# Stick-breaking attention in a two-block network: absolute values shared between two engines, query products over steps 2 to 18, one weight chunk rounded at the stage's end

## What is computed

```
q = split_heads(u @ attn_w_q[i])
z = jnp.einsum('bhqd,bhkd->bhqk', qb, kb) * scale
causal = s_pos < t_pos
log_beta = jax.nn.log_sigmoid(z)
log_one_minus = jnp.where(causal, jax.nn.log_sigmoid(-z), 0.0)
log_remain = lax.cumsum(log_one_minus, axis=3, reverse=True) - log_one_minus
weights = jnp.where(causal, jnp.exp(log_beta + log_remain), 0.0)
o = einsum('bhqk,bhkd->bhqd', weights, vb)
h = h + o @ attn_w_o[i]
```

## Time and profile before

| | us |
|---|---|
| median of 3 runs | 2513.57 (2511.74 to 2515.11) |
| the profiled execution, its own time | 2511.76 |
| its span | 2510.0 |
| PE busy | 2483.5 (99%) |
| DVE busy | 1027.2 (41%) |
| ACT busy | 735.6 (29%) |
| POOL busy | 974.5 (39%) |

### The profile page before, as it was taken

One profiled execution on the slowest core, in us unless ns is written; L12 is line 12 of the kernel. 1 busy time (PEld: TensorE's weight loads), 2 busy tenths in 40 slices (PEclk: granted clock), 3 DMA queues, 4 the chain that ended last, 5 costly groups with the idle time before them and its releaser, 6 DMA issues.

```text
span 2510.0 us, 30052 instructions
## 1 busy us (share of the span) xinstructions
PE 2483.5 (99%) x11638; PEld 1981.9 (79%) x11638; DVE 1027.2 (41%) x1489; ACT 735.6 (29%) x963; POOL 974.5 (39%) x305
## 2 busy tenths in 40 slices
PE   9999999999999999999999999999999999999998
PEld 7777887777888888568888888888888767888887
DVE  6363615458222317974223110422321686522301
ACT  3454225523222222242222222222122453222221
POOL 3322243204444442124444444444444663444442
PEclk9999999999999999999999999999999999999999
DMA  4222132212222233512222233322223211222232
GB/s 161 100 84 84 67 118 76 93 51 84 100 100 90 85 110 103 154 36 99 100 100 80 92 113 121 131 100 100 85 92 126 83 35 51 101 100 86 84 103 79
DMA packets 42752, 235.81 MB, mean 94 GB/s; under 512 B 5552, under 2 KB 5552, under 8 KB 22448
## 3 DMA queue, kind: packets, MB, share of 16 engines
q1 hardware_dynamic: 41808, 231.55, 26.9%
q10 hardware_dynamic: 864, 3.15, 0.3%
HBM read 222.86 MB, written 6.29 MB: 91 GB/s over the span
## 4 chain that ended last, share of the span: by engine, by line
PE 70%; DVE 3%; issue 3%; POOL 1%; ACT 1%; SPq 0%; DMA 0%; DVEq 0%; ACTq 0%; POOLq 0%
PE ps L1679 22%; PE ps L1680 22%; PE ps L1681 22%; PE ps L2069 1%; PE ps L2180 1%; PE ps L2160 1%; PE ps L2197 1%; PE ps L2186 1%; POOL w_lo L579 1%; DVE w_lo L1142 0%; DVE conv_out L1508 0%; SPq L543 0%; DVE tmp L1508 0%; PE ps L2170 0%; DVE tmp L1613 0%
## 5 line engine op out<-in xcount | busy, mean ns | idle before, releaser
L579 POOL TENSOR_TENSOR w_lo<-raw,w_hi 128x2048 fp32r<-128x2048 f32 (+1 forms) x204 | 863.7, 4234 | 1365.1 <-ACT w_hi L709 1342.7
L1679 PE MATMUL ps<-x_hi,w_hi 128*128 128x512 f32 x2047 | 809.3, 395 | 2.0 <-POOL w_lo L579 1.4
L1681 PE MATMUL ps<-x_hi,w_lo 128*128 128x512 f32 x2047 | 797.8, 390 | 0.0
L1680 PE MATMUL ps<-x_lo,w_hi 128*128 128x512 f32 x2047 | 797.5, 390 | 0.0
L1679 PEld LDWEIGHTS ps<-x_hi,w_hi 128*128 128x128 f32 x2047 | 384.6, 188 | 101.4 <-issue 20.8
L709 ACT ACTIVATE w_hi<-raw 128x2048 fp32r<-128x2048 f32 (+1 forms) x215 | 375.7, 1748 | 286.3 <-PE ps L1681 281.5
L1681 PEld LDWEIGHTS ps<-x_hi,w_lo 128*128 128x128 f32 x2047 | 384.5, 188 | 81.0
L1680 PEld LDWEIGHTS ps<-x_lo,w_hi 128*128 128x128 f32 x2047 | 384.9, 188 | 77.2 <-issue 0.7
L1189 DVE TENSOR_TENSOR tmp<-ps,rms_b 128x512 f32<-128x512 f32 x88 | 60.9, 691 | 585.4 <-PE ps L1681 582.4
L1681 PE MATMUL ps<-hid_hi,w_lo 128*128 128x512 f32 x704 | 273.9, 389 | 0.0
L1679 PE MATMUL ps<-hid_hi,w_hi 128*128 128x512 f32 x704 | 273.9, 389 | 0.0
(11 more groups left out here) (255 smaller groups left out, 2436.4 us busy)
## 6 DMA issues: line engine op xcount, KB each, us to landing
raw<-in_w_up SPq DMA_DIRECT2D x88, 1024.0 KB, 4.8
raw<-in_w_down SPq DMA_DIRECT2D x64, 704.0 KB, 4.0
raw<-in_w_feat SPq DMA_DIRECT2D x22, 1024.0 KB, 4.8
raw<-in_w_pw SPq DMA_DIRECT2D x12, 1024.0 KB, 5.1
raw<-in_w_tok SPq DMA_DIRECT2D x8, 1024.0 KB, 4.9
raw<-in_w_out SPq DMA_DIRECT2D x8, 1024.0 KB, 4.8
shifted<-conv_in SPq DMA_DIRECT2D x80, 67.5 KB, 2.0
bias<-in_bias_t SPq DMA_DIRECT2D x8, 512.0 KB, 5.9
```

The lines of the kernel that those rows point to most:

```text
L579: nc.gpsimd.tensor_tensor(w_lo[:, s, 0:w], raw[:, s, 0:w], w_hi[:, s, 0:w].bitcast(f32), ALU.subtract).then_inc(lo_ready, 1)
L1679: nc.tensor.matmul(out, hi, src_hi, start=start, stop=False, skip_group_check=True)
L1680: nc.tensor.matmul(out, hi, src_lo, start=False, stop=False, skip_group_check=True)
L1681: return nc.tensor.matmul(out, lo, src_hi, start=False, stop=stop, skip_group_check=True)
```

## The change

Four edits, all in the stick-breaking stage and its end:

1. ScalarE takes the absolute value of the second head of each step (`sb_second_absolute`, function Abs, out of PSUM), ahead of the two exponentials of that step and behind the weights where those come first. DVE keeps the first head's.
2. DVE rounds the softplus with a two-input instruction (t times 1, max t, both inputs the same tile) instead of a copy.
3. The 40 query products are dealt over steps 2 to 18, and the evictions in `Q_MOVED` move with them (query tiles 6 and 7 from steps 14 and 17 to 15 and 18).
4. The second chunk of w_o is no longer rounded in quarters during steps 18 to 23 (four of `sb_high`, four of `sb_low`). ACT and POOL do it whole after the stage, as elsewhere.

```diff
--- before.py
+++ after.py
@@ -149,11 +149,11 @@
 
 
 Q_STEPS = {}
-for _t in range(5):
-    Q_STEPS[3 * _t + 3], Q_STEPS[3 * _t + 4], Q_STEPS[3 * _t + 5] = 2, 3, 3
-Q_MOVED = {3 * _t + 5: _t + 3 for _t in range(5)}
+for _first, _products in ((2, (2, 2, 2, 2)), (6, (2, 3, 3)), (9, (2, 3, 3)), (12, (2, 2, 2, 2)), (16, (3, 3, 2))):
+    Q_STEPS.update((_first + _n, _count) for _n, _count in enumerate(_products))
+Q_MOVED = {5: 3, 8: 4, 11: 5, 15: 6, 18: 7}
 PIECES = 4
-SB_HIGHS = {6: 0, 8: 1, 9: 2, 10: 3, 12: 4, 13: 5, 15: 6, 16: 7, 18: 8, 19: 9, 21: 10, 22: 11}
+SB_HIGHS = {6: 0, 8: 1, 9: 2, 10: 3, 12: 4, 13: 5, 15: 6, 16: 7}
 SB_LOWS = {i + 1: n for i, n in SB_HIGHS.items()}
 
 
@@ -442,7 +442,7 @@
 
     def sb_piece(n):
 
-        name, c = (("q", 3), ("o", 0), ("o", 1))[n // PIECES]
+        name, c = (("q", 3), ("o", 0))[n // PIECES]
         at = CHUNK // PIECES * (n % PIECES)
         return first[name] + c, c % 2, slice(at, at + CHUNK // PIECES), n % PIECES == PIECES - 1
 
@@ -689,7 +689,8 @@
             if r == 2 and pair + 2 < SB_PAIRS:
                 stage_sb(pair + 2, 2)
                 stage_sb(pair + 2, 3)
-        pool.wait_ge(lo_ready, first["o"] + 2)
+        pool.wait_ge(lo_ready, first["o"] + 1)
+        low_part("o", 0, 1)
         low_parts("o", 1)
         low_parts("up3")
         low_parts("down3")
@@ -1005,16 +1006,24 @@
                 ins = nc.scalar.activation(stick[:, u % 4, 0:n], bank[:, 0:n], ACT.Exp)
             ins.then_inc(sb_exp, 1)
 
+        def sb_second_absolute(i):
+            u, n = 2 * i + 1, sb_width(i)
+            act.wait_ge(sb_z, u + 1)
+            if u >= 6:
+                act.wait_ge(sb_soft, u - 5)
+            nc.scalar.activation(tmp[:, u % 6, 0:n], ps[:, Z_BANK[u % 6], 0:n], ACT.Abs).then_inc(act_link, 1)
+
         def sb_decay(i, e):
-            u = 2 * i + e
-            t = tmp[:, u % 6, 0:sb_width(i)]
-            act.wait_ge(sb_abs, u + 1)
+            t = tmp[:, (2 * i + e) % 6, 0:sb_width(i)]
+            if e:
+                act.wait_ge(act_link, 3 * i + 1)
+            else:
+                act.wait_ge(sb_abs, i + 1)
             nc.scalar.activation(t, t, ACT.Exp, scale=-1.0).then_inc(act_link, 1)
 
         def sb_logs(i, e):
-            u = 2 * i + e
-            t = tmp[:, u % 6, 0:sb_width(i)]
-            act.wait_ge(act_link, u + 1)
+            t = tmp[:, (2 * i + e) % 6, 0:sb_width(i)]
+            act.wait_ge(act_link, 3 * i + e + 2)
             nc.scalar.activation(t, t, ACT.Ln, bias=1.0).then_inc(sb_log, 1)
 
         def sb_high(n):
@@ -1032,6 +1041,8 @@
             for e in range(2):
                 if short_arguments:
                     sb_weights(i - 2, e)
+            if i < steps:
+                sb_second_absolute(i)
             for e in range(2):
                 if i < steps:
                     sb_decay(i, e)
@@ -1046,7 +1057,7 @@
                     sb_logs(i, e)
             if i in SB_HIGHS:
                 sb_high(SB_HIGHS[i])
-        layer("o", squares_of_two("up3"), second_rounded=True)
+        layer("o", squares_of_two("up3"))
         feed_forward(3, "final")
         root_of("final")
 
@@ -1599,8 +1610,8 @@
         sb_query(1)
         sb_query(2)
 
-        def sb_absolute(i, e):
-            u, n = 2 * i + e, sb_width(i)
+        def sb_absolute(i):
+            u, n = 2 * i, sb_width(i)
             dve.wait_ge(sb_z, u + 1)
             if u >= 6:
                 dve.wait_ge(sb_soft, u - 5)
@@ -1622,7 +1633,9 @@
                            3: sb_step_of(pair - 1, 3) if pair else None}[SB_KIND[i]]
             if last_reader is not None:
                 dve.wait_ge(sb_arg, 2 * last_reader + 2)
-            nc.vector.tensor_copy(soft_of_step(i, e, False), tmp[:, u % 6, 0:sb_width(i)]).then_inc(sb_rounded, 1)
+            t = tmp[:, u % 6, 0:sb_width(i)]
+            nc.vector.scalar_tensor_tensor(out=soft_of_step(i, e, False), in0=t, scalar=1.0, in1=t, op0=ALU.mult,
+                                           op1=ALU.max).then_inc(sb_rounded, 1)
 
         def sb_output(pair):
 
@@ -1651,8 +1664,7 @@
             if i in Q_MOVED:
                 sb_query(Q_MOVED[i])
             if i < steps:
-                sb_absolute(i, 0)
-                sb_absolute(i, 1)
+                sb_absolute(i)
             if 1 <= i <= steps and not beside:
                 sb_softplus(i - 1, 1)
                 sb_rounds(i - 1, 1)
```

## The result

The changed kernel took 2519.32 us (median of 15 runs, 2517.02 to 2521.94), the kernel before 2513.91 beside it (15 runs, 2510.03 to 2515.82). The ratio is 1.0025 with a 95% interval of 1.0018 to 1.0031: **slower, by 5.4 us**. The forecast, 2509.8, had the wrong sign. Rival D named nearly this time, 2519.7, and part of the cause.

The account below looks back on a forecast made before the run. TensorE, busy for 99% of the span, bounds the kernel, so other engines count only where it waits. Head 1.2, middle -0.7 and tail 3.3 sum to 3.8 us off 2513.57: 2509.8, range 2505.5 to 2515.0.

Parts of the forecast that it names:

- Rival D: Slower rounding on the path in every step, 9.9 us for all 50: slower by 6.1, 2519.7; chance 0.12.
- The head: Two query products ahead of step 2's scores fill PE's wait: gain 1.2 us, between 0 and 1.36.
- 1.00 throughout: Sign that the forecast is right: PE's granted clock stays at 1.00 throughout.
- Edit 3, middle: Iterations 13 and 14 have one product less each, step 14's scores wait: loss about 0.7 us, at most 1.4.
- Edits 1 and 2, DVE: 25 absolute values leave DVE (14.4 us), slower roundings add 9.9: net 4.5 us less, in the middle on no path.
- step 20: In the tail, PE waits 1.6 us ahead of step 20's scores instead of 0.96.
- Edit 1, ACT: Absolute value at most 0.592 us: free in 256 and double steps, everything behind 0.5 us later in 512 steps.
- Edit 4: After the stage, rounding the second chunk of w_o whole has 5 us of cover before PE needs it: costs nothing.
- The tail, walked: From step 18's scores to the first product with w_o: 38.7 us against 41.9, gain 3.3.
- B: Clock falls again in the tail, where two waits of 1.6 and 1.8 us remain: gain 1.3, 2512.3; chance 0.23.
- C: In the tail, waits ahead of steps 20 and 23 vanish as well: gain 7.2 us, 2506.4; chance 0.20.

Follow-up runs that it names:

- {4}: Kernel before with only the second chunk of w_o rounded whole after the stage: 2509.31 us, ratio 0.9989 (0.9980 to 0.9998).
- {3,4}: Kernel before with the new dealing of products and the second chunk of w_o rounded whole after the stage: 2512.90 us, ratio 1.0006.
- the two kernels compared at step 18: {1,4}, and {4} with the second head's absolute value on ACT only outside the 512-column steps: 2511.82 and 2508.24 us.
- {3}: Kernel before with only the new dealing of products over steps 2 to 18: 2514.39 us, ratio 1.0004 (0.9995 to 1.0013).
- {1,4}: Kernel before with the second head's absolute value on ACT and the second chunk of w_o rounded whole after the stage: 2511.82 us, ratio 0.9991.

## Why the prediction was wrong, point by point

- **The head: the step that failed most.** "Gain between 0 and 1.36, I take 1.2", from edit 3, and nothing from edits 1 and 2; measured +5.8. The two products did fill the 1.08 us wait at step 2. But the step treated that wait as PE's alone. PE then waited 4.30 us at step 5, for a chain through ACT's and DVE's lists that the products do not feed. "PE arrives earlier at what they make" was written down, without a price: the walk of the lists made for the tail was not made for the head. In the full change it is the lesser part: counted from S0, PE came to step 5 only 0.5 us earlier than before (17.7 and 18.2), and ACT's weights 4.5 us later (21.9 and 17.5). The slower roundings on DVE's list do most of that, a term that the sum put at nothing in the head: without them the head is 2.4 us shorter, with the old dealing 0.6. On top of {4} it is the other way round, 1.2 for the rounding and 2.7 for the dealing. Of the 5.8 us, 4.8 are idle time and 1.7 the longer low clock, less 0.8 in the rest. A low clock of 3.4 us was in the head before too, from 1960.8 on, which the prediction did not look at when it asked for 1.00 throughout.
- **Edit 3, middle: right.** 0.7 forecast; 0.9 in {3,4}, with the wait at step 14 of 0.57 us that was expected there. In the full change the middle lost 1.7, with the rounding's 0.6 in it, and that wait was 1.1 us.
- **Edits 1 and 2, DVE: size right, place wrong.** Free roundings take 0.69 us at 512 columns (forecast 0.68), and DVE's busy time fell less than the 4.5 net: 1026.0 against 1027.2. The failed step is "each engine is held off by the other as before, and by 0.25 us longer". Here are the roundings of the kernel after in the stage, by shape:

```profile
L1637 DVE SCALAR_TENSOR_TENSOR soft_c_hi<-tmp 128x512 fp32r<-128x512 f32 x16 | 19.4, 1215 | 0.5
...
L1637 DVE SCALAR_TENSOR_TENSOR soft_b_hi<-tmp 128x512 fp32r<-128x512 f32 x14 | 10.3, 734 | 0.5
...
L1637 DVE SCALAR_TENSOR_TENSOR soft_a_hi<-tmp 128x256 fp32r<-128x256 f32 x16 | 10.1, 628 | 0.5
```

  Before, the means were 840, 448 and 509 ns: 0.38, 0.29 and 0.12 more each, 12 us in all instead of 9.9. That they lie on a path wherever PE has no products was counted in the tail walk with 0.3 us of drain and a share of the 0.6 ahead of step 20, and measured there at 2.5. "In the middle on no path" was nearly right: 0.6 us in 12 steps.
- **Edit 1, ACT: right in its parts, and the part was not priced on the path.** 0.60 us instead of 0.59, "everything behind comes 0.5 us later" in the 512 steps: 0.47. The sum nevertheless gave it nothing ahead of step 20. On top of {4} the tail is 2.4 us longer with the 512 steps, 1.7 of it the clock, and 1.1 shorter without them. The groups and waits of the kernel after:

```profile
L1014 ACT ACTIVATE tmp<-ps 128x512 f32<-128x512 f32 x15 | 9.0, 601 | 7.5 <-PE ps L2182 7.5
```
```profile
ACT tmp L1022 <- DVE tmp L1618: 25.5, 16, 3.9
```

  (the second row: total us, how many waits, the longest). ACT waits 25.5 us in the stage for DVE's half. The rule of the Trainium skill that the prediction weighed (page "ScalarE: Activation LUTs", section "Rules for kernel authors") names relu, max, min, add and mul for VectorE, not the absolute value. Taken as the prediction took it, the edit alone would lose; alone the edit was 0.9997 (0.9988 to 1.0006), no difference. In the two kernels compared at step 18 the place in ACT's list decides.
- **Edit 4: right.** Behind the stage 417.08 us against 417.12: the second chunk costs nothing there. It is the only edit whose gain is clear of noise, 3.9 us by the medians and 2.8 by the ratio, by the mechanism named (the quarter of 1.58 us ahead of step 21).
- **The tail, walked: 38.7 forecast, 40.80 measured.** Step 21 came without wait and step 23 waited 1.6 (forecast 1.8), the drain was 11.99 (11.8). The failed term is step 20: a wait of 2.43 where 1.6 stood, and behind it a low clock from 2071 on for 3.4 us. POOL's first staging piece was where the walk put it, 1.83 us behind step 18 (forecast 2.0):

```profile
2062.35 0.61 POOL L663 CAST sb_qk_hi<-sb_q 128x512 fp32r<-128x512 f32 x1 [5.71 <-DVE sb_q L1595]
```

- **The rivals.** B (the clock falls again in the tail) happened, for 3.4 us instead of 11. Its price is off by a little too: by the walk's own starts the gain between steps 21 and 24 is 3.0 us (16.0 before, 13.0 walked), not 2.5. C did not happen; its "DVE loses 2.5 us per three steps" leaves out the slower roundings, 1.3 us by the forecast's own prices. D had the time nearly right and a part of the mechanism: the rounding costs 4.7 us in the full change, in head and tail, not in every step, and the dealing comes on top. That D's time was met is luck: it took 9.9 us for 50 roundings off a gain of 3.8 that was not there, where the measured price is 4.7. DVE's busy share was no sign of it. In the tail's first stretch DVE was busier before the change (13.62 of 15.0 us) than after it (10.27 of 15.80), and the waits were longer after it: roundings of 1.25 to 1.7 us directly ahead of an absolute value weigh more than the share.

**Open.** What makes a low clock last 3.4 us in one run and 6.8 in the next with the same code, and why the dealing's price in the full change is 4.7 us by the medians and 2.8 by the profiled stages. An absolute value behind the exponentials of the 512 steps was not tried, nor other deals for the head.

## What to carry to other kernels

A wait that work is moved into is a gain only up to the next thing the engine needs: walk the lists of the engines that produce it, from the moved work to the next full wait, and count the cover that is missing where the work came from. On an engine with an in-order list a busy share of 40% says nothing: ask what stands directly between a result and the one who waits for it, and put added work where that engine itself waits. Price edits one by one on top of the one that frees the path, since an existing stall hides what the others cost.

## What the runs showed of the hardware

- **A two-input rounding pays more beside POOL.** Free it takes 0.69 us at 512 columns. Beside a POOL instruction it took up to 1.81, and nearly all such roundings of the stage ended 0.55 us after POOL's instruction; the copy of before ended 0.28 after it. A rounding of only 128 columns took 1.41 us at 1960.99, where the free copy took 0.23. The softplus and the absolute values, which read PSUM, kept their 0.68 and 0.41. The Trainium skill, page "SBUF — State Buffer", section "🔬 SBUF: two separate sides", has DVE instructions with two SBUF inputs and GpSimd's share a port pair as an exclusive lock, whole instructions at a time; the trace agrees. The copy is held off as well (up to 1.35 us), so the swap frees nothing, as forecast.
- **The low clock came in lengths of 3.4, 6.8 or 10.2 us**, and each began during a wait of PE of 1.05 us or more, or within 2 us of its end. The reverse does not hold. Waits of 0.93 and 0.95 us in the tail were not followed by one. Ahead of step 20, the wait of 1.99 in {3} was, those of 1.98 to 2.00 in three other kernels were not, and that of 2.19 in {1,4} was. Waits of 1.2 us there went either way too. Where it fell, matmul groups took longer: the 12 products with `neg_ones` behind the scores of step 5 took 2.81 us from 1983.04 on, against 1.62 in the middle of the kernel before.
- **The stage's start varies by up to 3.5 us** for identical code up to there: S0 at 1956.55 to 1957.32 in eight of the 17 profiles, at 1958.18 to 1958.67 in eight, at 1960.01 in one. The runs of one kernel spread over 2.5 to 8 us.
